# Regrouping the small TensorE jobs of the gated attention, and spreading the first key transposes, in a one-core hybrid decoder step

## The reference

```
(gq, gk, gv, glr, gg, pv, pg, fq, fk, fv, ff, fg) = split(rmsnorm(h, pre) @ w_in)
# gated linear attention, per chunk of 64 tokens and per head (6 heads, dk=32, dv=64)
a     = where(causal, qe @ ke.T, 0)                 # "scores"
o     = a @ v + qe @ s                              # "out"
s_new = exp(b_end) * s + (k * exp(b_end - b)).T @ v # "state"
# softmax attention with forgetting, per head of 64 channels
p = softmax(q @ k.T / 8 + F_t - F_s, causal)        # prompt: own keys; sample: cached pages and own keys
y = h + rmsnorm([gla * silu(gg) | pool * silu(pg) | fox * silu(fg)] @ w_out, post)
```

## Time and profile before

| | us |
|---|---|
| runs: median (lowest to highest) of 3 | 689.45 (688.36 to 690.57) |
| the profiled execution's own time | 691.41 |
| its span, first to last instruction | 689.8 |
| outside the span | 1.6 |
| PE busy | 658.8 (96%) |
| DVE, ACT, POOL busy | 392.4, 259.7, 145.1 |
| mean granted TensorE clock | 0.993 |
| chunks 10 to 13 of the projection with the gated attention | 156.2 to 240.3 |
| opening of the softmax attention | 398.8 to 412 |

### The profile page before, as it was taken

One profiled execution on the slowest core, in us unless ns is written; L12 is line 12 of the kernel. 1 busy time (PEld: TensorE's weight loads), 2 busy tenths in 40 slices (PEclk: granted clock), 3 DMA queues, 4 the chain that ended last, 5 costly groups with the idle time before them and its releaser, 6 DMA issues.

```text
span 689.8 us, 13243 instructions
## 1 busy us (share of the span) xinstructions
PE 658.8 (96%) x5183; PEld 566.9 (82%) x5183; DVE 392.4 (57%) x714; ACT 259.7 (38%) x479; POOL 145.1 (21%) x165
## 2 busy tenths in 40 slices
PE   6999999999999999999999989998999889999996
PEld 6889999899999889999999965766667655688884
DVE  5845926473455305159999967335443458654543
ACT  7536542121111436221112064745564557332321
POOL 3262202111111001223312040123222201121210
PEclk9999999999999899999999999999999999999999
DMA  7412103311110032354120282557666533113132
GB/s 236 140 40 62 31 8 70 84 39 32 33 32 2 4 85 87 78 160 119 31 62 0 85 262 78 161 169 217 184 209 180 175 133 107 44 64 123 61 123 91
DMA packets 59735, 67.29 MB, mean 98 GB/s; under 512 B 14156, under 2 KB 49883, under 8 KB 59673
## 3 DMA queue, kind: packets, MB, share of 16 engines
q1 hardware_dynamic: 54505, 51.37, 25.1%
q0 software_dynamic: 5168, 15.08, 7.3%
HBM read 57.71 MB, written 8.68 MB: 96 GB/s over the span
## 4 chain that ended last, share of the span: by engine, by line
PE 83%; DVE 7%; ACT 5%; issue 2%; DMA 1%; POOL 0%; SPq 0%; DVEq 0%; ACTq 0%; POOLq 0%
PE PS L1898 14%; PE PS L1899 14%; PE PS L1900 13%; PE PS L1791 4%; PE PS L1792 4%; PE PS L1793 4%; PE PS L2185 3%; PE PS L2167 3%; PE PS L2120 3%; PE PS L2142 2%; PE PS L2085 2%; PE PS L2072 2%; DVE rows_odd L1670 2%; DVE YF L1549 1%; PE PS L2211 1%
## 5 line engine op out<-in xcount | busy, mean ns | idle before, releaser
L1898 PE MATMUL PS<-xh,wh 128*128 128x368 f32 x576 | 197.0, 342 | 0.8 <-POOL wl L636 0.5
L1899 PE MATMUL PS<-xl,wh 128*128 128x368 f32 x576 | 190.9, 331 | 0.0
L1900 PE MATMUL PS<-xh,wl 128*128 128x368 f32 x576 | 190.5, 331 | 0.0
L636 POOL TENSOR_TENSOR wl<-wr,wh 128x1024 fp32r<-128x1024 f32 x24 | 61.7, 2570 | 264.5 <-ACT wh L1011 264.5
L1898 PEld LDWEIGHTS PS<-xh,wh 128*128 128x128 f32 x576 | 108.7, 189 | 4.9 <-issue 1.5
L1899 PEld LDWEIGHTS PS<-xl,wh 128*128 128x128 f32 x576 | 108.8, 189 | 0.9
L1900 PEld LDWEIGHTS PS<-xh,wl 128*128 128x128 f32 x576 | 108.8, 189 | 0.0
L617 DVE TENSOR_TENSOR wr<-wr,small 128x1024 f32<-128x1024 f32 x24 | 35.8, 1493 | 40.3 <-DMA wr<-in_w_in_dram 40.2
L1529 DVE RECIPROCAL RA<-RA 128x1104 f32<-128x1104 f32 x8 | 56.4, 7053 | 0.3
L1791 PE MATMUL PS<-woh,yh 128*128 128x512 f32 x128 | 50.5, 395 | 0.0
L1793 PE MATMUL PS<-woh,yl 128*128 128x512 f32 x128 | 50.2, 392 | 0.0
(11 more groups left out here) (327 smaller groups left out, 1120.6 us busy)
## 6 DMA issues: line engine op xcount, KB each, us to landing
wr<-in_w_in_dram SPq DMA_DIRECT2D x24, 512.0 KB, 3.9
kpage<-in_cache_fox_k_dram SPq DMA_DIRECT2D x64, 192.0 KB, 2.8
RA<-in_cache_fox_v_dram POOLq DMA_DIRECT2D x32, 192.0 KB, 3.5
pagesB<-in_cache_fox_v_dram POOLq DMA_DIRECT2D x32, 192.0 KB, 3.5
YF<-in_x_prompt_dram SPq DMA_DIRECT2D x8, 512.0 KB, 6.9
xres<-in_x_prompt_dram SPq DMA_DIRECT2D x8, 512.0 KB, 3.9
out_y_p_dram<-zout SPq DMA_DIRECT2D x16, 256.0 KB, 2.1
wo_raw_a<-in_w_out_dram SPq DMA_DIRECT2D x6, 512.0 KB, 5.6
```

What stands on the lines that cost most here:

```text
L636: eng.tensor_tensor(low, wr[:, c % 2, :, 0:m], wh[:, c % 2, :, 0:m].bitcast(F32), ALU.subtract).then_inc(wlo_done, 1)
L1898: pe.matmul(out, high, xh[:, k, cols], start=(k == 0), stop=False)
L1899: pe.matmul(out, high, xl[:, k, cols], start=False, stop=False)
L1900: ins = pe.matmul(out, low, xh[:, k, cols], start=False, stop=(k == KT - 1))
```

## The change

In `side_jobs` the cuts of the list move from 10, 20, 28 to 10, 21, 31: chunk 11 takes `out 4` too, chunk 12 takes ten jobs instead of eight, and chunk 13 six instead of nine. In `project_in`, where the next job is one of the sample jobs, it is given alone and not in a pair. In the plan's opening two `page_kT` follow the first exponentials instead of three; one follows each of the three P1 pieces of the blocks 2 and 3; the last follows the first two T units. `sample_queries()` moves to the place of that last one.

```
-        s[9 + c] = gla[(0, 10, 20, 28)[c]:(10, 20, 28, len(gla))[c]]
+        s[9 + c] = gla[(0, 10, 21, 31)[c]:(10, 21, 31, len(gla))[c]]
...
+ALONE = ("sample_q", "sample_scores", "sample_out", "sample_state")
...
-    late = []
+    late, keys = [], sample_keys(0)
...
-    order += late + sample_keys(0)[:3]
+    order += late + keys[:2]
     late = []
-    for u in scored(0, 1):
+    for n_, u in enumerate(scored(0, 1)):
         items, exps = score(*u)
-        order += items
+        order += items + keys[2 + n_:3 + n_]
         late += exps
-    order += sample_keys(0)[3:]
+    keys = keys[2 + len(scored(0, 1)):]
...
+            order, keys = order + keys, []
             order += BEHIND_TURNS.get(units[first], [])
...
-                elif key == ("page_kT", 0, 0, 0):
+                elif key == ("page_kT", 0, 1, 2):
                     sample_queries()
...
                         if upto < len(jobs):
-                            upto -= (upto - given) % 2
+                            alone = upto > given and jobs[given][0] in ALONE
+                            upto = given + 1 if alone else upto - (upto - given) % 2
```

## The result

The changed kernel takes 693.47 us (median of 5 runs, 692.55 to 695.01) against 689.45 us (688.36 to 690.57): a ratio of 1.0054, 95% interval 1.0038 to 1.0071. Two further measurements beside before gave 1.0064 (1.0046 to 1.0081) and 1.0045 (1.0030 to 1.0061). The forecast was 689.9 in a range of 687.2 to 691.9 and a ratio within 0.3%; it was too low by 3.6 us.

What follows compares the result with a forecast made beforehand. The prediction took TensorE, busy for 96% of the span, as the bound. For the median run, clock -1.5, groups +0.4, waits +2.2 and opening -0.65 summed to +0.45 us, giving 689.9 us, range 687.2 to 691.9.

Steps and rivals of the forecast that it cites:

- The jobs themselves are the same and are only moved: Side jobs in chunks 10 to 13: their own matmuls cost no more after the change, so no term.
- the +0.45 of the sum: Whole kernel, median run: clock -1.5, groups +0.4, waits +2.2 and opening -0.65 give +0.45 us, 689.9 us.
- Groups: Projection, chunks 10 to 13: 21 groups of jobs instead of 19, each costing 0.19 us beside its matmuls, +0.4 us.
- Waits: TensorE ahead of `out` jobs in chunks 10 to 13: `out 4` 1.07 us, three others 0.37 each; together +2.2 us.
- Opening: Start of the softmax attention: T units of block pair 1 come earlier, -0.65 us, bounds 0 and -1.2.
- Clock: End of chunk 13: the half-clock fall from 236.5 us goes, -3.0 us in the profiled execution, -1.5 in the median.
- Cost taken 0: Chunk 10: `sample_q` given alone loses no clock, 0 us, though its margin is not visible.
- The rule weighed in the prediction: Clock term: regrouping that removes no idle gap returns nothing, 0 us; not followed, kept as a rival's value.
- the third: Rival, chunks 10 to 13: the clock does not come back, +1.95 us, 691.4, up to +3 with a second fall; 20%.
- the sum for the profiled execution: Whole kernel, profiled execution: -3.0 + 0.4 + 2.2 - 0.65 = -1.05 us, from 691.41 to 690.4.

Runs made afterwards that it cites:

- states_apart: Kernel before the change, but in chunks 10 to 13 the second of two states due together comes one projection step later; ratio 1.0047, 693.77 against 690.49 us.
- after_state_first: The changed kernel, but VectorE drains an odd state first and makes the masked queries behind it; ratio to the kernel before 1.0040.
- grouped_open: Kernel before with the changed opening, cuts at 10, 20, 30 and side jobs grouped by kind, no states parted; ratio 0.9992, 689.06 against 690.05 us.
- before_look: The kernel before, unchanged, one more profiled execution; chunks 10 to 14 last 101.57 us with a clock fall of 3.4 us.
- after_again: The changed kernel, unedited, timed and profiled once more; 694.52 us, chunks 10 to 14 in 105.93 us with a clock fall of 3.4 us.
- open_only: Kernel before with only the opening of the softmax attention changed, side jobs as before; ratio 0.998, 690.10 against 690.91 us.
- before_look3: The kernel before, unchanged, another profiled execution; its clock fell at 465.8 us, no total time given.

## Why the prediction was wrong, step by step

- *"The jobs themselves are the same and are only moved"*: this step failed, and it carries most of the miss (2.2 of the 3.3 us between the +0.45 of the sum and the +3.7 of the ratio; the clock below carries most of the rest). I priced a lone state as half of a pair, 0.19 us; it takes 0.34. Five pairs of states are parted by the new lists, +1.5 us. An `out` that ends its group lasts 1.50 instead of 1.40 us and a `scores` that begins one 0.99 instead of 0.94, +0.7 in all. Together 2.2 us that the sum had at 0. states_apart shows the price of a lone state without waits or moved jobs, and after_state_first the whole 2.2 with the waits taken out.
- *Groups:* +0.4 as said; grouped_open has 21 groups and nothing else new, and lasts 0.4 us longer.
- *Waits:* +2.2 predicted, 1.6 measured. `out 4` waited 1.1 us as said. The three others were 0.15 each and not 0.37: TensorE came to `out` 0.3 us later than I reckoned, because each of the two lone states ahead of it took 0.15 us longer. The price that I had missed covered the wait that I had found.
- *Opening:* -0.65 predicted, -0.45 measured. The changes came where they were expected: TensorE waits 0.24 us for ScalarE's key copy and no longer for VectorE, and the copies of the sample's queries lie behind the second T unit (409.87) with no cost. The lines of the changed kernel that answer to the earlier trace rows:

```profile
406.42 0.66 PE L2077 MATMUL PS<-ident,kpage 128*128 128x128 f32 x4 [0.24 <-ACT kT L1268]
...
409.31 1.03 ACT L1262 ACTIVATE PT<-PS 128x1024 f32<-128x1024 f32 x1 [0.28 <-PE PS L2172]
...
409.87 1.24 DVE L1661 COPY q_diag<-YF 64x64 f32<-64x64 f32 x6
410.23 0.59 ACT L1268 ACTIVATE kT<-PS 128x512 f32<-128x512 f32 x1
...
413.53 0.71 PE L2172 MATMUL PS<-ident,rows_odd 128*16 128x128 f32 x5 [0.75 <-ACT rows_odd L1211]
```

  The stage begins 2.01 us later here than in before. ScalarE's first copy begins 0.94 us sooner relative to it, and the key copy of 0.5 us that now lies between it and the exponentials takes half of that.
- *Clock:* for the profiled execution -3.0 was right to 0.1: the fall at 236.5 was gone, and the timed executions bear the mechanism out (0 of 75 against 22 of 117). For the median the term was -1.5, half of an unknown. As what before loses it was about right, by luck: 1.4 us on average by the table of clocks (690.6 less the 689.1 of executions without a fall). What failed is *"Cost taken 0"* for `sample_q` alone: the changed kernel loses clock too, 1.5 us behind `sample_q` in two of five profiles, and 0.4 us on average by the table. So the change returned 1.0 us at most, and not 1.5. (The profiles alone would say 1.7, 2.3 lost in these chunks against 0.6, but three of the four of before were of the worst kind.)

  Without clock the change costs 4.4 - 0.45 = 3.9 us. The three measurements show +3.7, +4.4 and +3.1 us, a return of 0.2 on average, and by their intervals anything from -1.7 to +1.8. They differ the way their clocks do: with +4.4 the mean clocks were 0.9967 in before and 0.9958 in the changed kernel, with +3.1 0.9965 and 0.9973; for the first, those of before are not on record. What stays open is the difference between a return of 0.2 and one of 1.0.
- *The rule weighed in the prediction,* of the Trainium skill, page "TensorE: Matmul & The Clock Gate", section "Why this matters for your kernels": it says that throughput drops are avoided by leaving no idle gaps between bursts of matmuls. The trace does not agree: the falls whose stretch ahead is shown (before_look, after_again) came with TensorE busy for all of it, so a gap is not needed. In open_only and before_look3 the clock also fell at 465.8 us, and there TensorE had been idle for part of the stretch ahead, in before_look3 for 1.70 of 3.80 us:

```profile
462.00:465.80 3.80, 2.10 (x18) 1.06 (x18) 1.80 (x9) 1.41 (x3) 1.64 (x4) 1.00 0.91 265
```

  The first execution of before was idle for 1.13 us in this stretch and kept its clock. So the rule may hold at that place, which no run here tests; it does not describe the falls in chunks 10 to 13. As a forecast of the result the value 0 that the rule gave was nearer than mine.
- *The rivals:* the third, that the clock does not come back, came nearest by its time (691.4, more with a second fall), but not by its mechanism: what it said would stay (the fall at the end of chunk 13) went.

With the job prices put in (+2.2) and the waits and the opening as measured, the sum for the profiled execution is -3.1 + 0.4 + 1.6 + 2.2 - 0.45 = +0.65. With the later landing of the first input rows (+0.7), which has nothing to do with the change, it is +1.35; the page shows +1.5, and the 0.2 between them lies in the projection, which took 1.7 us more where the groups and the wait ahead of `out 4` account for 1.5.

## What to carry to other kernels

The cost of a small matmul job is not its own: measure it in the company it will have. Where an order is changed that keeps every job, list for each job what stood before and behind it and look for a row of it alone; a pair's half is a lower bound and not a price. And a rule that takes one item out of a paired list, or a cut at an odd place, shifts all pairs behind it (1.5 and 2.8 us here); grouping by kind spread the sample jobs for 0.4. Where the clock varies, sort the timed executions by their mean granted clock before a few profiles are taken for the usual case.

## What was not expected of the hardware

- Twelve matmul records of a state (64 rows, 32 columns of weights, 64 columns moved) hold TensorE for 0.34 us alone and 0.38 us for 24 of them: nearly all of the 0.34 is paid once for a row of states, not once for each.
- The granted clock falls at different jobs in different executions of the same program, at 164.5 and 236.8 us in two executions of before, each time to 0.50 and for 3.4 or 6.8 us, in these chunks with TensorE at work for all of the stretch ahead where this was read. By the mean clocks 25 of 83 executions of before had no fall at all.
- With the clock taken out, stages agree between executions to 0.04 us in 140 and 0.06 in 270. Times a tenth of a microsecond apart can be read from one profile, where runs need differences of 1 us.
